# Hybrid decoder step with a routed expert layer: how the router's sums are formed, when the spilled rows' operations run, and filler products on TensorE

## What is computed

```
h = h + hierarchical_moe(rms_norm(h, norm_ffn_g), ...)
gate = sigmoid(rms_norm(h, norm_ple_g) @ w_ple_gate)
h = h + (p @ w_ple_proj) * gate

def hierarchical_moe(c, w_rg, b_rg, w_re, b_re, w_gate, w_up, w_down):
    gl = xf @ w_rg + b_rg;  gp = softmax(gl);  g = argmax(gl)          # 4 groups
    el = (xf @ w_re + b_re).reshape(-1, 4, 4);  el_g = el[group g]     # 4 experts in each
    top_v, top_i = top_k(el_g, 2);  w = softmax(top_v) * gp[g]
    for e in range(16):
        y = y + combine[:, e:e+1] * ((silu(xf @ w_gate[e]) * (xf @ w_up[e])) @ w_down[e])
```

## Time and profile before

| | |
|---|---|
| time, median of 3 runs | 612.93 us (612.31 to 615.21) |
| the profiled execution | 616.3 us, its span 614.5 us |
| busy in the span: PE / DVE / ACT / POOL | 575.9 / 501.7 / 357.4 / 201.6 us |
| mean granted clock of PE | 0.976 of full |
| DMA | 147.16 MB, mean 239 GB/s |
| mixers, up to the first router transposes | about 0 to 180 us |
| router, up to the gathered rows | about 180 to 227 us |
| expert steps | about 231 to 532 us |
| tail | about 532 to 614 us |

### The profile page before, as it was taken

One profiled execution on the slowest core, in us unless ns is written; L12 is line 12 of the kernel. 1 busy time (PEld: TensorE's weight loads), 2 busy tenths in 40 slices (PEclk: granted clock), 3 DMA queues, 4 the chain that ended last, 5 costly groups with the idle time before them and its releaser, 6 DMA issues.

```text
span 614.5 us, 9357 instructions
## 1 busy us (share of the span) xinstructions
PE 575.9 (94%) x3185; PEld 479.2 (78%) x3185; DVE 501.7 (82%) x570; ACT 357.4 (58%) x378; POOL 201.6 (33%) x219
## 2 busy tenths in 40 slices
PE   5799999999999888899999999999999999869994
PEld 3799987987887666688888888888888888557783
DVE  5678997998644775888999999999999997978576
ACT  6541434335635627577777787777778785623256
POOL 8153864996200010043222122122212322221123
PEclk9799999999999799899999999999999999979998
DMA  9978120116342318689999999999999996880004
GB/s 251 290 218 291 69 69 13 57 62 215 105 176 86 139 47 315 241 306 362 382 386 375 369 394 381 385 386 380 392 355 392 400 341 218 276 301 1 1 2 154
DMA packets 74917, 147.16 MB, mean 239 GB/s; under 512 B 10012, under 2 KB 21884, under 8 KB 74431
## 3 DMA queue, kind: packets, MB, share of 16 engines
q1 hardware_dynamic: 68133, 132.69, 60.8%
q0 software_dynamic: 5008, 9.55, 4.2%
q10 hardware_dynamic: 1746, 4.53, 2.2%
HBM read 140.70 MB, written 14.00 MB: 252 GB/s over the span
## 4 chain that ended last, share of the span: by engine, by line
PE 75%; DVE 12%; DMA 4%; issue 3%; ACT 3%; POOL 2%; SPq 0%; POOLq 0%; ACTq 0%; DVEq 0%
PE pair L2038 20%; PE pair L2040 19%; PE pair L2039 19%; PE pair L2109 7%; PE pair L2057 3%; DVE pair L1490 2%; DVE lo L1427 2%; PE pair L2097 2%; DMA h<-in_x_prompt 1%; PE pair L2047 1%; PE pair L2048 1%; DMA raw<-pairs 1%; ACT hi L984 1%; PE pair L2425 1%; DMA pairs<-wide,conv 1%
## 5 line engine op out<-in xcount | busy, mean ns | idle before, releaser
L1427 DVE TENSOR_TENSOR lo<-raw,hi 128x2048 fp32r<-128x2048 f32 x104 | 235.8, 2290 | 50.5 <-ACT hi L984 49.6
L984 ACT ACTIVATE hi<-raw 128x2048 fp32r<-128x2048 f32 (+1 forms) x114 | 215.0, 1902 | 58.9 <-PE pair L2040 34.2
L2038 PE MATMUL pair<-hi,act 128*128 128x512 f32 (+1 forms) x580 | 233.3, 402 | 4.9 <-DVE lo L1427 2.6
L2040 PE MATMUL pair<-hi,act 128*128 128x512 f32 (+1 forms) x580 | 226.8, 391 | 0.0
L2039 PE MATMUL pair<-lo,act 128*128 128x512 f32 (+1 forms) x580 | 226.4, 390 | 0.0
L2038 PEld LDWEIGHTS pair<-hi,act 128*128 128x128 f32 (+1 forms) x580 | 109.8, 189 | 33.3 <-DVE lo L1427 4.5
L2040 PEld LDWEIGHTS pair<-hi,act 128*128 128x128 f32 (+1 forms) x580 | 109.5, 189 | 24.1
L2039 PEld LDWEIGHTS pair<-lo,act 128*128 128x128 f32 (+1 forms) x580 | 109.8, 189 | 21.2
L984 ACT ACTIVATE act<-pair 128x1024 fp32r<-128x1024 f32 (+3 forms) x50 | 37.8, 772 | 64.4 <-PE pair L2057 39.6
L878 POOL DMA_INDIRECT pairs<-two,few x15 | 39.0, 2600 | 102.8 <-DVE two L1769 102.8
L1490 DVE SCALAR_TENSOR_TENSOR pair<-conv,vecs,pair 128x512 f32<-128x512 f32 x104 | 69.6, 749 | 0.0
(11 more groups left out here) (293 smaller groups left out, 580.8 us busy)
## 6 DMA issues: line engine op xcount, KB each, us to landing
raw<-in_w_exp_gate SPq DMA_DIRECT2D x32, 1024.0 KB, 10.3
raw<-in_w_exp_up SPq DMA_DIRECT2D x32, 1024.0 KB, 10.3
raw<-in_w_exp_down SPq DMA_DIRECT2D x32, 1024.0 KB, 11.7
h<-in_x_prompt SPq DMA_DIRECT2D x8, 512.0 KB, 7.2
raw<-in_w_in SPq DMA_DIRECT2D x8, 512.0 KB, 7.5
raw<-in_w_in SPq DMA_DIRECT2D x4, 1024.0 KB, 8.7
raw<-in_w_out SPq DMA_DIRECT2D x4, 1024.0 KB, 8.0
raw<-in_w_ple_gate SPq DMA_DIRECT2D x4, 1024.0 KB, 8.6
```

The costliest lines, as they stand in the source:

```text
L984: return nc.scalar.activation(out_, in_, ACT.Copy)
L1427: nc.vector.tensor_tensor(lo[:, n % SPLIT, :], raw[:, n % RAW, :], hi[:, n % SPLIT, :].bitcast(F32), ALU.subtract).then_inc(lo_dve, 1)
L2038: mm(out_, x_hi, w_hi, start=start, stop=False)
L2040: return mm(out_, x_lo, w_hi, start=False, stop=stop)
```

## The change

On VectorE the running sums and the total are gone; `onehot` is signalled as soon as M is complete. TensorE forms them itself: besides the triangular product it multiplies `ones` by the tables of the earlier tiles, shifted by one, two, three and four tiles, into the same accumulation, and later the five tables of M into the counts. `rank_ps` is now signalled twice, and POOL waits for the second. The embedding products are halved, so that the ranks come behind tile 0 and the first half of tile 1; the second half follows the ranks, and tiles 2 and 3 both follow the lists. VectorE's six operations for the weights stand behind the writing of the lists. `spill_picks`, `spill_list` and `spill_lists` each come ten steps later, and the loops are cut accordingly: TensorE's runs over steps 2 to 11, VectorE's over 3 to 10, the rest is written out. A new helper, `keep_clock`, issues exact products of the identity with itself, 128x128, whose result nobody reads: 5, 1 and 2 in the router, 7 behind step 0, 3, 18 and 3 in the tail.

```diff
+PICK_STEP = 10
@@ gpsimd
-            g.wait_ge(rank_ps, 1)
+            g.wait_ge(rank_ps, 2)
@@ vector, router
-            link(nc.vector.memset(M[SAMPLE:, full, :], 0.0))
-
-            link(nc.vector.memset(earlier[:, 0, :], 0.0))
-            for t in range(1, TILES):
-                link(nc.vector.tensor_tensor(earlier[:, t, :], earlier[:, t - 1, :], M[:, t - 1, :], ALU.add))
-            nc.vector.tensor_tensor(spare2[:, 0, :], earlier[:, full, :], M[:, full, :], ALU.add).then_inc(onehot, 1)
-
-            v.wait_ge(exp_done, 2)
-            link(nc.vector.tensor_reduce(gsum, egl, AX_X, ALU.add))
-            link(nc.vector.reciprocal(gw, gsum))
-            link(nc.vector.tensor_scalar(den, diff, 1.0, None, ALU.add))
-            link(nc.vector.reciprocal(den, den))
-            link(nc.vector.tensor_tensor(w1, den, gw, ALU.mult))
-            link(nc.vector.tensor_tensor(w2, w1, diff, ALU.mult))
+            nc.vector.memset(M[SAMPLE:, full, :], 0.0).then_inc(onehot, 1)
@@ vector, experts
+            v.wait_ge(exp_done, 2)
+            link(nc.vector.tensor_reduce(gsum, egl, AX_X, ALU.add))
+            link(nc.vector.reciprocal(gw, gsum))
+            link(nc.vector.tensor_scalar(den, diff, 1.0, None, ALU.add))
+            link(nc.vector.reciprocal(den, den))
+            link(nc.vector.tensor_tensor(w1, den, gw, ALU.mult))
+            link(nc.vector.tensor_tensor(w2, w1, diff, ALU.mult))
             split_low(N_MOE + 1)
             gather_low(0)
             step(0)
-            spill_picks()
             step(1)
             step(2)
+            with v.Fori(0, PICK_STEP - 2) as d:
+                step(3, d)
+            spill_picks()
+            step(PICK_STEP + 1)
+            step(PICK_STEP + 2)
             spill_lists()
-            with v.Fori(0, STEPS - 4) as d:
-                step(3, d)
+            for e0 in range(PICK_STEP + 3, STEPS - 1):
+                step(e0)
@@ tensor
+            def keep_clock(to, n):
+                for _ in range(n):
+                    mm(to[:, 0:P], ident[:, :], ident[:, :], start=True, stop=True)
...
+            keep_clock(bank[0], 5)
             router_parts(TILES - 2)
             router_rows(TILES - 1)
+            keep_clock(bank[7], 1)
             router_logits(TILES - 2)
+            keep_clock(bank[7], 2)
             router_parts(TILES - 1)
...
             embedding(0)
-            embedding(1)
+            embedding_half(1, 0)
             pe.wait_ge(onehot, 1)
-            mm(bank[5][:, 0:TILES * EXPERTS], before[:, :], M.rearrange(flat), start=True, stop=False)
-            mm(bank[5][:, 0:TILES * EXPERTS], ones[:, :], earlier.rearrange(flat), start=False, stop=True)
-            mm(bank[5][:, P:P + EXPERTS], ones[:, :], r16[:, 5, 0, :], start=True, stop=True).then_inc(rank_ps, 1)
-            embedding(2)
+            mm(bank[5][:, 0:n], before[:, :], M, start=True, stop=False)
+            for t in range(1, TILES):
+                ins = mm(bank[5][:, t * EXPERTS:n], ones[:, :], M[:, 0:n - t * EXPERTS], start=False, stop=(t == TILES - 1))
+            ins.then_inc(rank_ps, 1)
+            embedding_half(1, 1).then_inc(pp_ps, 1)
             for k in range(2):
                 for t in range(TILES):
                     pe.wait_ge(picked, TILES * k + t + 1)
+                    if (k, t) == (1, 0):
+                        for i in range(TILES):
+                            ins = mm(bank[5][:, P:P + EXPERTS], ones[:, :], M[:, i * EXPERTS:(i + 1) * EXPERTS],
+                                     start=(i == 0), stop=(i == TILES - 1))
+                        ins.then_inc(rank_ps, 1)
...
+            embedding(2)
             embedding(3)
...
             pe.wait_ge(pp_sb, TILES)
+            keep_clock(bank[6], 7)
             step(1)
+            with pe.Fori(0, PICK_STEP) as d:
+                step(2, d)
             spill_list()
-            with pe.Fori(0, STEPS - 3) as d:
-                step(2, d)
+            for e0 in range(PICK_STEP + 2, STEPS - 1):
+                step(e0)
...
+            keep_clock(bank[3], 3)
             last_product(0)
             last_product(1)
+            keep_clock(bank[4], 18)
             pe.wait_ge(head_norm, 1)
             head_rows(0, head_ps)
+            keep_clock(bank[4], 3)
```

22 lines of the change are left out of this document (12 added, 10 removed).

## The result

The changed kernel takes **620.3 us** (median of five executions, 614.7 to 620.8), the kernel before beside it 613.0. Forecast were 610.3 us and a range of 607.6 to 613.3, so the kernel is slower where I expected it faster or the same, though by how much, 0.4 to 1.2%, differs between series. The five executions are not alike: the profiled one took 614.7 at a mean granted clock of 0.984, the other four 620.1 to 620.8 at 0.973 to 0.975.

A forecast was written before the change was run, and what follows sets the result against it. TensorE was taken to bound the kernel (75% of the chain of waits), with gains only where it waits or runs at its lower clock. -0.7 - 3.65 + 2.2 - 0.45 = -2.6 from 612.93 gave 610.3 us, range 607.6 to 613.3.

The forecast's parts named there:

- The router: Router: sums moved from VectorE to TensorE gain 0.7 us; bounds a gain of 1.4 and a loss of 0.8.
- the wait of 2.16 is gone: Router: TensorE's wait before the transposes of the first gathered rows disappears, as part of the 0.7 us gain.
- The router's fillers: Router: eight fillers, 0.26 us each, lie in TensorE's waits before the embedding products and cost nothing.
- Rival (a): New waits in router and eleventh step cost the clock, 1.5 us once, 3.0 twice: 611.8 to 613.3; chance 0.19.
- Rival (c): Fillers do not keep the clock and stand in the way, at 0.5 us each: +7.0, 619.9; chance 0.05.
- The second expert: Second expert: without `spill_picks` there, TensorE's 2.43 us wait goes and the clock gives 1.2; gain 3.65 us.
- The eleventh step: Eleventh step: `spill_picks` there makes TensorE wait before its third unit; 2.2 us lost.
- Rival (d): Eleventh step hides the picks, because ScalarE is late there by a load: 607.8 to 608.5; chance 0.16.
- rival (b): Expert steps: DMA loads set the pace, so part of the gain is lost: 611.4 or 612.4; chance 0.10.
- The tail: Tail: 24 fillers in TensorE's waits keep the clock up for the transposes; gain 0.45 us, bounds 0 and 0.8.

The follow-up runs named there:

- no_fill: The changed kernel without any of its fillers (router 8, second expert 7, tail 24); ratio to the kernel before 0.9997.
- no_router_fill: The changed kernel without the router's eight fillers, those of the second expert and tail kept; ratio to the kernel before 0.9972.
- pause_fill: The changed kernel without the router's eight fillers and with eight fillers in the eleventh step's wait; ratio to the kernel before 0.9992.
- sums_only: The kernel before with only the router's new sums, embedding order and later weights operations, no fillers; ratio to the kernel before 1.0012.
- order_only: The kernel before with one move, embedding(2) behind the lists instead of ahead of them; ratio to the kernel before 1.0045.
- again: The changed kernel once more, nothing edited, in twelve executions; ratio to the kernel before 1.0040, executions 614.4 to 620.4 us.
- no_router_fill_2: The changed kernel without the router's eight fillers, measured a second time; ratio to the kernel before 0.9984.
- onehot_fill: The changed kernel plus eight more fillers ahead of TensorE's wait for `onehot`; ratio to the kernel before 0.9968.
- fill_and_break: The changed kernel plus eight fillers in the `onehot` wait and the first half of embedding(2) between the list products; ratio to the kernel before 0.9985.
- move_only: The kernel before with only the spilled rows' operations moved ten steps along, no fillers; ratio to the kernel before 0.9987.

## Why the prediction was wrong

The step that failed is the router's: -0.7, at worst +0.8, with its eight fillers put at nothing. The router came out at +2.1 us in the first trace and +5.2 in the second, and taking the fillers out gives back 0.56 to 0.68% (3.4 to 4.2 us). The other parts came as forecast.

**The router, -0.7 forecast.** The sum was right for an undisturbed clock: it gave 226.8 - 202.04 = 24.8 us for the router's length, and it is 24.5 in the four traces in which no fall lies behind the sums (no_fill, no_router_fill, pause_fill, sums_only). In the mean of executions even that gain does not show (sums_only, +0.7). What failed is the bound on the other side, "a loss of 0.8 if the clock falls in the new 1.9 us wait (1.5 us of slower products)". The fall came; the wait was 2.13. But it took two stretches in the first trace (router +2.1) and 13.6 us in the second (+5.2), and two things had gone unweighed. A fall need not end after 3.4 us, nor does it need a standstill ahead of it. And "the wait of 2.16 is gone" was booked as the gain that it looks like, not as the loss of what had absorbed falls; order_only has 2.8 us for that, together with TensorE's new wait for VectorE's tables.

**The router's fillers, "the fillers lie in waits", nothing.** They are cheap, 7 in 1.73 us or 0.25 each, where I took 0.26, and they do keep the clock (1.00 over the embedding products in the first trace, 0.50 before). The step that failed is the question of what then waits: I had TensorE 1.9 us early at `onehot` in my own working and went on, with fillers that speed up only what then stands still. Between `again` and no_router_fill, on the same chip, they cost 0.68%, 4 us, and against no_router_fill_2, on another, 0.56%.

**Rival (a)** was the right mechanism with 0.19, and its price of 3.0 for two falls was too low: in `again` the router is 6.2 us over the 24.5 of an undisturbed one, and the fall behind the eleventh step's wait adds 1.5. **Rival (c)** came near the measured time (619.9) by the wrong way, which is luck: of the larger groups only the tail's 18 took more than its 0.28 us each (5.31 us, 0.295 each, in part at half clock). The transposes behind them start 0.4 us late (541.68, VectorE's rows are ready at 541.23), and the next are in time.

**The second expert, -3.65.** Right, and a little more: -4.3 (18.97 us between the transposes at 242.21 and 261.18 before, 14.71 after), wait gone and clock at 1.00. For the clock I took 1.2 because the timed runs might have no fall there: the six traces with the wait of 2.4 us all have one behind it, the fourteen with the move none.

**The eleventh step, +2.2.** Right: one wait of 2.10. In the other traces it is up to 2.39. The clock fell behind it in three of the twelve traces in which it is not filled (`again`, onehot_fill, fill_and_break). Rival (d) is out, and so is rival (b): ScalarE's waits for loads, six of `w_exp_down` between 400 and 500 before, are none after. Its waits from 400 to 500 (us in total, times, longest):

```profile
ACT hi L985 <- PE pair L2039: 10.3, 12, 2.7
ACT act L985 <- PE pair L2061: 10.0, 6, 1.7
ACT act L985 <- PE pair L2443: 6.2, 5, 1.2
```

**The tail, -0.45.** Right in the trace: transposes at 0.66, VectorE's operation with 0.78 instead of 1.23 of waiting.

**The median.** I took before's distance between profiled execution and median (3.4) over to the changed kernel. There it was 5.6 the other way. The 613 us of before was itself low: its medians beside the other kernels are 615.5 to 615.9.

## What to carry to other kernels

Before shortening work or adding fillers on the bounding engine, ask what it will wait for next: time won ahead of a wait is a standstill, and a clock that is low over uncritical products may be better than one that is low later (no_router_fill 0.9972, `again` 1.0040). A short wait behind such a place is not only waste; it can take up what varies ahead of it (in move_only the wait shrank from 2.16 to 0.51 and the router stayed at 25.2 us, 25.5 before). And a change that moves where the clock falls should be judged by many executions (three to five of them misled me here), with one trace of a long one.
